# A feed-forward layer computed by seven block products of halves (Strassen) in place of eight

## The reference

```python
D_MODEL = 1024
D_FF = 4 * D_MODEL
    ...
    x = x + merged @ w_out
    h = _rmsnorm(x, norm2_w)
    x = x + jnp.square(jax.nn.relu(h @ w_up)) @ w_down
```

## Time and profile before

| what | value |
|---|---|
| time, median of 3 runs | 2838.57 us (2838.07 to 2839.18) |
| span of the profiled execution, first to last instruction | 2834.8 us |
| mean granted TensorE clock, share of full speed | 0.983 |
| busy share of the span: PE, DVE, ACT, POOL | 96%, 56%, 36%, 7% |
| first matmul of the feed-forward | 2081.47 us |
| from 2081.40 us to the end: length | 753.40 us |
| in it: PE, DVE, ACT, POOL busy | 748.57, 320.77, 102.01, 0.00 us |
| in it: granted clock, DMA | 1.00, 56 GB/s |

### The profile page before, as it was taken

The page is one execution under the profiler, slowest core; times in us unless marked ns, Lnnn a source line. Parts: engine busy times, 40 slices in busy tenths (PEclk is TensorE's granted clock), DMA queues, the critical chain, the costliest instruction groups (busy, mean ns, idle before and its releaser), DMA issues. The chain is left out here.

```text
span 2834.8 us, 47428 instructions
## 1 busy us (share of the span) xinstructions
PE 2717.8 (96%) x18594; PEld 2642.7 (93%) x18594; DVE 1578.1 (56%) x2975; ACT 1007.8 (36%) x2302; POOL 207.6 (7%) x299
## 2 busy tenths in 40 slices
PE   5999989999999999989999989998989999999999
PEld 5999889999999999979999989998989999999999
DVE  5433536566566566557998845454363444444434
ACT  4333336556655656653343422112221111111110
POOL 0000000000000000004555510000000000000000
PEclk8999999999999999999999989999989999999999
DMA  4332353343343343328888854333221111111112
GB/s 161 122 122 76 107 156 101 96 124 101 90 128 104 90 134 97 92 84 193 210 200 211 203 157 141 120 121 125 70 89 45 45 45 45 45 47 54 50 56 97
DMA packets 326606, 308.72 MB, mean 109 GB/s; under 512 B 66480, under 2 KB 283056, under 8 KB 326256
## 3 DMA queue, kind: packets, MB, share of 16 engines
q1 hardware_dynamic: 326384, 305.69, 37.1%
HBM read 218.32 MB, written 87.28 MB: 108 GB/s over the span
## 5 line engine op out<-in xcount | busy, mean ns | idle before, releaser
L411 PE MATMUL banks<-w_hi,xn_hi 128*128 128x256 f32 x1440 | 408.3, 288 | 5.0 <-DVEq L368 5.0
L411 PE MATMUL banks<-w_lo,xn_hi 128*128 128x256 f32 x1440 | 403.4, 284 | 0.0
L414 PE MATMUL banks<-xn_hi,w_hi 128*128 128x352 f32 x1152 | 380.2, 330 | 11.9 <-ACTq L352 7.3
L414 PE MATMUL banks<-xn_hi,w_lo 128*128 128x352 f32 x1152 | 379.6, 330 | 0.0
L414 PE MATMUL banks<-xn_lo,w_hi 128*128 128x352 f32 x1152 | 379.3, 329 | 0.0
L411 PE MATMUL banks<-w_hi,xn_lo 128*128 128x256 f32 x1280 | 364.0, 284 | 0.0
L411 PEld LDWEIGHTS banks<-w_hi,xn_hi 128*128 128x128 f32 x1440 | 274.9, 191 | 6.6 <-DVEq L368 5.1
L411 PEld LDWEIGHTS banks<-w_lo,xn_hi 128*128 128x128 f32 x1440 | 274.5, 191 | 0.1
L1857 PE MATMUL banks<-h_hi,w_hi 128*128 128x352 f32 x768 | 248.9, 324 | 2.5 <-DVEq L1778 2.5
L1857 PE MATMUL banks<-h_hi,w_lo 128*128 128x352 f32 x768 | 248.7, 324 | 0.0
L1857 PE MATMUL banks<-h_lo,w_hi 128*128 128x352 f32 x768 | 248.7, 324 | 0.0
(11 more groups left out here) (282 smaller groups left out, 5903.2 us busy)
## 6 DMA issues: line engine op xcount, KB each, us to landing
w_raw<-in_w_in SPq DMA_DIRECT2D x44, 1024.0 KB, 5.9
scratch_xbc<-att_co SPq DMA_DIRECT2D x32, 512.0 KB, 2.9
ssd_ab<-scratch_acum SPq DMA_DIRECT2D x64, 256.0 KB, 5.9
br_g<-scratch_gates SPq DMA_DIRECT2D x72, 176.0 KB, 3.8
scratch_gates<-hand_tanh SPq DMA_DIRECT2D x48, 176.0 KB, 5.4
att_k<-scratch_k_hi SPq DMA_DIRECT2D x64, 128.0 KB
scratch_z<-att_z_stage SPq DMA_DIRECT2D x64, 128.0 KB, 2.0
ssd_xbc<-scratch_xbc SPq DMA_DIRECT2D x64, 128.0 KB, 3.4
```

The source lines that it names most:

```text
L411: ins = self.nc.tensor.matmul(self.bank(n, P, PW), x[:, k, t * P:(t + 1) * P], w[:, k, :], start=first, stop=end)
L414: ins = self.nc.tensor.matmul(self.bank(n, P, TT), w[:, k, m * P:(m + 1) * P], x[:, k, r * TT:(r + 1) * TT], start=first, stop=end)
```

## The change

The three matrices of each product are cut into halves both ways (hidden and inner dimension, and the 1056 tokens into 2 x 528), and a 2 x 2 block product is made from seven products of sums of blocks where the plain way takes eight. The names: A11 to A22 are the four quarters of the moving operand, S1 to S4 sums of them (S1 = A21 + A22, S2 = S1 - A11, S3 = A11 - A21, S4 = A12 - S2), and T1 to T4 the sums of weight quarters (T5, T6, T7, T4 in the code are numbered by the product that uses them). A product 1 to 7 takes one of the quarters or sums from either side; the results are again added up in twos and threes.

- **Up.** 16 panels of 256 hidden columns x 7 products of 24 matmuls (4 blocks, three passes, two column halves of 264). The seven moving operands are split once, at the start (`x_high`, `x_low`); the weights of a product are split as they are needed, through a ring of 10. GpSimd makes the four T sums of each panel. The first two panels are interleaved (OPENING), the others run in the order STEADY. The results are combined by VectorE (`take`), squared relu is one VectorE instruction (`activate`), and it is stored to HBM (`u_d`).
- **Down.** 4 slices of 1024 hidden rows x 7 products ("units") of 4 blocks of 128 outputs x 24 matmuls of 264 columns. Each slice loads its four quarters of u (1.08 MB each) back from HBM and its four quarters of w_down (1 MB each); GpSimd makes six of the eight sums and VectorE two (`second_s`, `second_t`); both operands of a unit are split one unit ahead (`down_high`, `down_low`). VectorE adds each result of a unit onto the sum of its product number (`collect`); in the last slice the seven sums are combined to the four output quarters, turned and added to x2 in 20 pieces. PSUM has three slots of two banks for the units.
- **Around it.** `out_norm` writes the turned rows unsplit (ScalarE's copy, into `merged`), and the split of the first w_up panel at its end falls away. The memset of the sums falls away.

The diff, cut:

```diff
+                    for i, _, _, bank in halves(t):
                         act.wait_ge(turned, i + 1)
-                        nc.scalar.activation(hi[:, blocks, cols], bank, ACT.Copy).then_inc(t_hi, 1)
+                        if t < NT:
+                            nc.scalar.activation(quarter(t // 4, i % 2)[:, :, t % 4 * P:(t % 4 + 1) * P], bank, ACT.Copy).then_inc(kept, 1)
...
-                if t is not None:
-                    for i, blocks, cols, bank in halves(t):
-                        dve.wait_ge(t_hi, i + 1)
-                        nc.vector.tensor_tensor(lo[:, blocks, cols], bank, hi[:, blocks, cols].bitcast(F32), ALU.subtract).then_inc(t_lo, 1)
...
+    HB = KB // 2
...
+    PANELS, SLICES = FF // PW, FF // D
...
+    OPENING = [(0, 1), (1, 1), (0, 2), (1, 2), (0, 5), (0, 6), (0, 7), (0, 4), (0, 3), (1, 6), (1, 5), (1, 7), (1, 4), (1, 3)]
+    STEADY = [1, 6, 2, 7, 5, 4, 3]
+    order = OPENING + [(p, n) for p in range(2, PANELS) for n in STEADY]
...
+    RING, FIRST, AHEAD = 10, 4, 8
...
+    DOWN = [1, 2, 6, 7, 4, 5, 3]
...
+        turns_after = {(LATE + 4, 0): [0], (LATE + 4, 1): [1], (LATE + 4, 2): [2], (LATE + 4, 3): [3], (LATE + 5, 0): [4],
+                       (LATE + 6, 0): [5, 6], (LATE + 6, 1): [7, 8], (LATE + 6, 2): [9, 10], (LATE + 6, 3): list(range(11, 20))}
...
+            def store_u(g):
...
+                sp.wait_ge(u_made, g + 1)
+                sp.dma_start(u_d[p * PW + k * P:p * PW + (k + 1) * P, i * HT:(i + 1) * HT], c_out[g % CR][:]).then_inc(u_stored[g % CR], 16)
+
+            def load_a(s, q):
+                i, j = q // 2, q % 2
...
+                    for k in range(CR):
+                        sp.wait_ge(u_stored[k], 16 * 4)
+                else:
...
+            load_up(1)
+            ready = {max(place[p, n] for n in (1, 2, 3)): p + 2 for p in range(PANELS - 2)}
+            for i, (p, n) in enumerate(order):
...
+                if i and order[i - 1] in result_no:
+                    store_u(result_no[order[i - 1]])
+                if (p, n) == (PANELS - 1, 6):
+                    sp.wait_ge(w_lo, done_at(PANELS - 2, 3))
...
+                    load_a(0, A11)
+                    load_a(0, A12)
+                    sp.wait_ge(w_lo, STEPS)
+                    load_b(0, "12")
+                    load_b(0, "21")
+            sp.wait_ge(up_done, done_at(PANELS - 1, 7))
+            load_a(0, A21)
+            load_a(0, A22)
+            sp.wait_ge(up_done, STEPS)
...
+            def panel_sums(p):
...
+                sub(tsum[5][:], b12, b11).then_inc(t_made[5], 1)
+                pool.wait_ge(t_made[5], p + 1)
+                sub(tsum[6][:], b22, tsum[5][:]).then_inc(t_made[6], 1)
+                sub(tsum[7][:], b22, b12).then_inc(t_made[7], 1)
+                pool.wait_ge(t_made[6], p + 1)
+                sub(tsum[4][:], b21, tsum[6][:]).then_inc(t_made[4], 1)
+            panel_sums(0)
+            pool.wait_ge(s_made, 1)
+            sub(quarter[A21], quarter[A11], quarter[A21]).then_inc(s3_made, 1)
+            pool.wait_ge(s_made, 2)
+            pool.wait_ge(x_lo, made_at[2])
+            sub(quarter[A12], quarter[A12], s2[:]).then_inc(s4_made, 1)
...
+            for s in range(SLICES):
+                pool.wait_ge(b_loaded["11"], 16 * (s + 1))
+                pool.wait_ge(b_loaded["12"], 16 * (s + 1))
...
+                    pool.wait_ge(up_done, done_at(PANELS - 1, 1))
+                sub(b_sum[:], b_raw["12"][:], b_raw["11"][:]).then_inc(dt1, 1)
...
+                    pool.wait_ge(up_done, done_at(PANELS - 1, 5))
+                add(a_sum[:], a_raw[A21][:], a_raw[A22][:]).then_inc(ds1, 1)
...
+                sub(a_raw[A21][:], a_raw[A11][:], a_raw[A21][:]).then_inc(ds3, 1)
...
+                sub(b_raw["12"][:], b_raw["22"][:], b_raw["12"][:]).then_inc(dt3, 1)
+                pool.wait_ge(d_lo, 2 * (7 * s + W_AT[2] + 1))
...
+                sub(b_raw["21"][:], b_raw["21"][:], b_raw["11"][:]).then_inc(dt4, 1)
...
+                sub(a_raw[A12][:], a_raw[A12][:], a_raw[A11][:]).then_inc(ds4, 1)
+            pool.wait_ge(taken, FP4 * (LATE + W_AT[2] + 1))
+            add(acc[2][:], acc[1][:], acc[2][:]).then_inc(first_sum, 1)
+            pool.wait_ge(taken, FP4 * (LATE + W_AT[5] + 1))
+            pool.wait_ge(u4_made, 1)
+            add(acc[5][:], acc[7][:], acc[5][:]).then_inc(c22_made, 1)
...
+                copy(xh[n][:], x_source[n]).then_inc(x_hi, 1)
...
+            def unit_high(i):
...
+                elif i >= FIRST:
+                    act.wait_ge(x_lo, len(MADE))
+                copy(wh[i % RING][:], w_source(p, n)).then_inc(w_hi, 1)
...
+            def keep_first(p):
+                act.wait_ge(up_done, done_at(p, 1))
...
+                copy(two(r1[p % 2][:]), both(slot_of(p, 1))).then_inc(r1_made, 1)
...
+            x_high(1)
+            unit_high(0)
+            unit_high(1)
+            x_high(2)
+            unit_high(2)
+            unit_high(3)
...
-            nc.vector.memset(acc[:], 0.0).then_inc(cleared, 1)
...
+            def unit_low(i):
+                dve.wait_ge(w_hi, i + 1)
+                tensor(wl[i % RING][:], w_source(*order[i]), wh[i % RING][:].bitcast(F32), ALU.subtract).then_inc(w_lo, 1)
...
+            def activate(g):
+                _, p, n = results[g]
+                c = c_out[g % CR][:]
+                dve.wait_ge(c_read[n], p + 1)
+                nc.vector.scalar_tensor_tensor(out=c, in0=c, scalar=0.0, in1=c, op0=ALU.max, op1=ALU.mult).then_inc(u_made, 1)
...
+            def down_low(u):
+                n, k = DOWN[u % 7], u % 2
+                dve.wait_ge(d_hi, 2 * u + 1)
+                tensor(ul[k][:], a_of[n][:], uh[k][:].bitcast(F32), ALU.subtract).then_inc(d_lo, 1)
+                dve.wait_ge(d_hi, 2 * u + 2)
+                tensor(dl[k][:], b_of[n][:], dh[k][:].bitcast(F32), ALU.subtract).then_inc(d_lo, 1)
...
+                tensor(b_raw["11"][:], b_raw["22"][:], b_sum[:], ALU.subtract).then_inc(dt2, 1)
+
+            def second_s(s):
+                dve.wait_ge(ds1, s + 1)
+                dve.wait_ge(ds3, s + 1)
+                dve.wait_ge(d_lo, 2 * (7 * s + 1))
+                tensor(a_raw[A11][:], a_sum[:], a_raw[A11][:], ALU.subtract).then_inc(ds2, 1)
...
+            def collect(u, f):
...
+                dve.wait_ge(d_done, at + 1)
...
+                    nc.vector.tensor_copy(x, both(at % 3)).then_inc(taken, 1)
+                else:
+                    dve.wait_ge(taken, FP4 * (u - 6))
+                    tensor(x, both(at % 3), x, ALU.add).then_inc(taken, 1)
...
+            x_low(1)
+            unit_low(0)
+            unit_low(1)
+            x_low(2)
+            unit_low(2)
+            unit_low(3)
+            tensor(s1[:], quarter[A21], quarter[A22], ALU.add).then_inc(s_made, 1)
+            dve.wait_ge(s_made, 1)
+            tensor(s2[:], s1[:], quarter[A11], ALU.subtract).then_inc(s_made, 1)
+            x_low(5)
+            x_low(6)
+            x_low(7)
+            x_low(4)
+            activate(0)
+            activate(1)
+            x_low(3)
+            for i in range(FIRST, STEPS):
+                for unit in fresh[i]:
+                    unit_low(unit)
+                if i > FIRST and order[i - 1] in result_no:
+                    p, n = order[i - 1]
+                    if not (p < 2 and n == 5):
...
+                if order[i] == (PANELS - 1, 5):
+                    down_low(0)
...
+                if u + 1 < U and u != 1:
+                    down_low(u + 1)
+                for f in range(FP4):
+                    collect(u, f)
...
+                        elif idx == 6 and s + 1 < SLICES:
+                            second_s(s + 1)
+                    elif f == 2 and idx == 6 and s + 1 < SLICES:
+                        second_t(s + 1)
+                if u == 0:
+                    second_s(0)
+                    second_t(0)
...
+            def product(p, n):
+                i = place[p, n]
+                pe.wait_ge(w_lo, i + 1)
+                pe.wait_ge(x_lo, made_at[n])
...
+                elif n == 7:
+                    pe.wait_ge(v_made, p + 1)
+                elif n == 4:
+                    pe.wait_ge(w_made, p + 1)
...
+                for a, (x, y, k) in enumerate(passes):
+                    for c in range(2):
+                        ins = nc.tensor.matmul(bank(slot_of(p, n), c), y[:, k, :], x[:, k, c * HC:(c + 1) * HC],
...
+            def down(u, f):
+                at, n, r = FP4 * u + f, DOWN[u % 7], u % 2
+                if f == 0:
+                    pe.wait_ge(d_lo, 2 * (u + 1))
+                if at >= 3:
+                    pe.wait_ge(taken, at - 2)
...
+                for a, (x, y, k) in enumerate(passes):
+                    for c in range(2):
+                        ins = nc.tensor.matmul(bank(at % 3, c), y[:, k, cols], x[:, k, c * HC:(c + 1) * HC],
...
-                        for c, (x, w, k) in enumerate(passes):
```

(95 more changed lines are left out.)

521 lines of the change are left out of this document (352 added, 169 removed).

## The result

The changed kernel takes 2846.26 us (median of 9 runs, 2843.13 to 2851.04), the kernel before 2838.36 (9 runs): 1.0027 of before, with an interval of 1.0017 to 1.0037. It is slower by 0.27%, where a gain of 0.48% was forecast.

The account below looks back on a forecast made before the run. TensorE's column stream was taken as the bound. Up ends at 2439.8, down adds 372.0 and the end 9.5: 2821.3, 13.5 under the old span of 2834.8; 2838.6 - 13.5 = 2825.0 us, range 2784 to 2845.

Parts of the forecast that it names:

- matmul of 264 columns: TensorE's stream: 123.4 ns each, 5376 in place of 4608 of 352 columns, a gain of 76.6 us.
- begin to fifth product: Feed-forward's start: operand splits and sums on VectorE and GpSimd add up by the port, 40.0 us; 31 without blocking.
- border of the parts, idle and clock: Up to down: late quarter loads and sums delay the first units by 16 us, plus 2.4 for TensorE's slow clock.
- three slice borders: Down part: VectorE's sums and low parts meet GpSimd's sums, 4.3 us a border, 13 in all.
- the port's rule: VectorE and GpSimd: port held a whole instruction, and VectorE's stream keeps it until VectorE waits; 2112-element GpSimd sums cost 4.7 us.
- The prices of the other engines: Prediction's section on VectorE, ScalarE and GpSimd operation times and their blocking; 2112 elements: VectorE 2.36 us, GpSimd 4.7.
- the rival of strict turns: VectorE lets GpSimd in after each operation: slice border 10 us, border of the parts 22, time 2848; chance 0.15.
- The other reading of the same section: VectorE and GpSimd: whoever has the port keeps it for a whole instruction; seen at 0.6 us, none shown at 4.7.
- the clock: TensorE starts slowly after a pause, at a granted clock of 0.50: 2.4 us for each such start.
- a pair spares nothing: Matmul stream: a weight block used twice in a row gives no gain; rival of spared loads 2789, chance 0.03.
- The waits of the first panels: OPENING, up part: products 7 and 4 stand right behind those they wait for, 3 x 0.75 = 2.3 us.
- The begin: Normalisation ahead of the feed-forward: dropped low parts let it begin 5.6 us earlier, at 2075.3 (bounds 0 and 8.4).

## Why the prediction was wrong

By its own steps, each with what the profiled execution showed:

| step | predicted | measured |
|---|---|---|
| matmul of 264 columns | 123.4 ns | 122.1 |
| GpSimd's sum of 2112 | 4.7 us | 4.74 to 4.78 undisturbed |
| begin to fifth product | 40.0 | 39.4 |
| from there to the end of up | 324.5 | 326.1 |
| border of the parts, idle and clock | 18.4 | 18.9 + 7.6 |
| three slice borders | 13 | 20.6 + 7 |
| all of down to the last matmul | 372.0 | 391.7 |
| from there to the end | 9.5 | 10.2 |
| feed-forward in all | 746.0 | 767.5 |

**The failed step is the port's rule in "The prices of the other engines".** I read "VectorE's stream keeps it until VectorE waits" out of one stretch in which two VectorE operations passed one of GpSimd, and gave the rival of strict turns 0.15 for it. In the feed-forward it is turns: at the border shown above the first low part of a unit stood behind what was left of one sum and the second behind the whole of the next, where my rule would have let the second pass. That is the rival's mechanism. It had priced a slice border at 10 and the border of the parts at 22, time 2848; measured were some 9.2 and 26.5, time 2846.26. That these lie so near is in part luck: the idle time alone was 6.85 and 18.9, and the rest is the slow clock below, for which the rival has no term of its own. The other reading of the same section, that each blocks the other for a whole instruction, held at 4.7 us as at 0.6; the Trainium skill's rule (SBUF — State Buffer, section "SBUF: two separate sides"), an exclusive lock for the whole instruction, agrees: a low part of 2.28 took 6.76. Why the stretch of the earlier trace rows went otherwise stays open. In the feed-forward of the changed kernel and of its ten variants no waiting operation of GpSimd is passed by two of VectorE that read SBUF twice, nor one of VectorE by two of GpSimd. But the profile of before has a still wider case in the state-space stage, without the idle time that GpSimd had ahead of it in the earlier trace rows (GpSimd, then VectorE):

```profile
1337.03 1.69 POOL L2612 TENSOR_TENSOR ssd_xdt<-ssd_xb,keep_dt 128x256 f32<-128x256 f32 x1
```

```profile
1337.11 1.12 DVE L2642 SCALAR_TENSOR_TENSOR ssd_L<-ssd_ab,keep_acum,maskT 128x128 f32<-128x128 f32 x4
```

GpSimd's operation of 0.61 us took 1.69 while four short ones of VectorE went by. So strict turns are what the feed-forward's operations show, and not a rule for every stretch.

**A second term was too small: the clock.** I charged 2.4 us once at the start of each part. But TensorE's clock falls after other waits too. Windows behind the waits of 7.4 and 5.35 us, and behind one of 1.49 (engines' busy time, then granted clock, DMA share, GB/s):

```profile
2494.10:2500.50 6.40, 6.33 (x29) 6.33 (x30) 6.36 (x6) 0.00 (x0) 0.00 (x0) 0.52 0.81 287
2546.30:2552.30 6.00, 5.99 (x30) 5.99 (x31) 1.66 (x3) 0.41 (x1) 1.44 (x1) 0.57 0.92 323
2585.80:2591.80 6.00, 6.00 (x49) 6.00 (x50) 2.59 (x4) 2.71 (x2) 0.00 (x0) 1.00 0.92 325
```

30 matmuls are worth 30 x 0.122 = 3.7 us and took 6.0: 2.3 more behind each wait of 5.35, nothing behind 1.49. At each slice border that makes 5.35 + 2.3 + 1.5 = 9.2, for 4.3 (all three have waits of 5.3 to 5.4 and of 1.5 to 1.6). At the border of the parts 29 matmuls in 6.4 lose 2.9; the two other restarts there (24 matmuls in 5.60 from 2481.20, and the first products from 2451.19) lose 2.7 and 2.0. In sum the idle time at these borders was 39.5 us where I had 29, and the clock took 14.6 where I had 2.4: the two weigh about alike, and the clock's share follows the waits.

**Right were** the step of the matmul, the price of GpSimd's sums, the start of 40 us, that TensorE doesn't wait in the up part's steady panels, and the view that a pair spares nothing. The waits of the first panels were 5.6 idle in place of 2.3: one product 7 waited 2.9, not 0.75.

**The begin.** The stage ahead of the feed-forward became shorter as I had said, from 126.5 us in the first profile to 121.8 (119.7 to 122.1 in the seven variants that leave it alone); 5.6 less was predicted. In the profiled execution it doesn't show, as that one came to the stage 5.4 us late, the open point above. In the medians it does: the feed-forward is 13.6 us longer and the whole only 7.9, and the 5.7 between them agree with the stage, 120.7 on the mean of the eight profiles with the old order for 126.4 in the two of before. The 3.8 us between span and median that I kept are not a distance within one execution (1.7 to 1.9 in every run); the forecast hangs on the difference of two spans and doesn't change by it.

So the gain of the stream was right and even larger (83.6 for 76.6), but the losses were put 28 us too low. The feed-forward came out 21.5 us longer than forecast, 19.7 of them in the down part. My range ended at 2845, 3 below the 2848 that I had worked out for strict turns, and the measured 2846.26 lies just outside it: a rival of 0.15 should have been inside.

## What to carry to other kernels

Count an operation that is "moved to an idle engine" by what it does to the busy one: on GpSimd a sum costs VectorE up to its whole length at each of VectorE's operations with two SBUF inputs that meets it. Without the down part's sums, and so without the waits for them to be made, the kernel was 53 us faster, where its matmul stream had won 84. No run put those sums on VectorE, so which engine is the better place for them isn't shown. Cut such sums into pieces no longer than what VectorE can wait for; the same work in four pieces turned a loss of 0.3% into a gain of 0.7%. And when a gain is taken from an engine that runs without a gap, price each new wait with the slow clock behind it.

## What the runs showed of the hardware

- In the feed-forward VectorE and GpSimd took strict turns, instruction by instruction: a low part of 2.28 us takes 6.76 beside whole sums of 4.5 to 4.8 and 3.41 beside pieces of 1.3, while an operation with a bank as one input keeps its 0.69 to 0.71. In the state-space stage four short VectorE operations (1.12 us together) passed one of GpSimd, which took 1.69 in place of 0.61; what decides between the two isn't shown.
- Undisturbed, GpSimd needs 1.29 us for 512 elements and 4.74 to 4.78 for 2112; cutting a sum into four costs it 5.0 to 5.2 in all when VectorE leaves it alone.
- After a wait of 5.35 us TensorE's granted clock over the next 6 us was 0.57 (30 matmuls), after one of 1.49 it stayed 1.00 (49 matmuls).
- A weight block that is used for two matmuls in a row gave 122.1 ns a matmul, and used once 121.5, with a weight load for every matmul in both.
